# Memory's mean squares taken once, during the first projections, and kept; memory's tiles split over both output units

## The chip, the cores and the metric

The kernel runs on one core of one Trainium2 chip. The time is the device time of one launch in microseconds (us), the median over several runs. Engines are named as the profile names them: PE is TensorE's matmul queue, PEld its weight loads, DVE VectorE, ACT ScalarE, POOL GpSimd, SP the engine that issues the DMAs.

## What is computed

Two layers of an encoder on 512 tokens of width 1024. Each has a token mixer (differential attention in layer 0, dilated attention in layer 1), a cross attention into 256 memory tokens, and a squared-ReLU MLP. Every sub-layer is normalised before and after:

```python
def rms_norm(x, g):
    xf = x.astype(jnp.float32)
    y = xf * lax.rsqrt(jnp.mean(xf * xf, axis=-1, keepdims=True) + NORM_EPS)
    return (y * g.astype(jnp.float32)).astype(x.dtype)

def memory_cross_attention(h, mem, mem_g, wq, wkv, wo):
    ...
    mn = rms_norm(mem, mem_g)
    q = (h @ wq).reshape(B, S, H, Dh)
    kv = (mn @ wkv).reshape(B, M, 2, H, Dh)
    ...

for i in range(DEPTH):
    h = rms_norm(x, mix_pre_g[i])
    ...                                   # mix = the layer's token mixer
    x = x + rms_norm(mix, mix_post_g[i])
    h = rms_norm(x, xa_pre_g[i])
    x = x + rms_norm(memory_cross_attention(h, mem, mem_g[i], xa_wq[i], xa_wkv[i], xa_wo[i]), xa_post_g[i])
    h = rms_norm(x, ffn_pre_g[i])
    x = x + rms_norm(squared_relu_mlp(h, w_up[i], w_down[i]), ffn_post_g[i])
```

`mem` is the same in both layers; only its gain `mem_g[i]` and the weights `xa_wkv[i]` differ. So the mean square of each memory token is the same number in both layers.

## The kernel before, in words

Activations lie with features on the 128 partitions: eight tiles of 128 features, by 512 tokens (256 for memory). Every product of a weight is made in three matmuls of split operands (high part by high part, and the two cross terms), so each weight and each activation is split: ACT rounds it into a high part (a *head*: `heads_of`, L608, for weights), and DVE subtracts that from the original for the low part (a *rest*: `rests_of`, L1021).

Work on weights is cut into *units* of 512 output columns. A unit has four *pairs* (0 to 3); a pair is two feature tiles of the weight, 512 KB, loaded by one DMA of SP into one of four slots of `raw`. For one pair PE runs 2 x 4 x 3 = 24 matmuls of 128x512 (12 in the two first units on memory, which have two banks of 128 tokens). Before a pair PE waits for its rest. A unit leaves four PSUM banks, which ACT or DVE evacuates while PE is at the next unit (units alternate between banks 0 to 3 and 4 to 7).

The units in order: `qkv0` (6 units, the *projections* of layer 0, numbered 0 to 5 here), then differential attention, `o0` (2 units, the first and the second *output unit*), `kv0` (4 units on memory: two make values, two keys), `xq0`, cross attention, `xo0`, the MLP, and then layer 1 the same with its own projections (`qkv1a`, `qkv1b`), `o1`, `kv1`, and so on.

There is no scheduler: each engine's program is written out by hand, one after the other, and runs strictly in that order; engines meet only at semaphores. In ACT's and DVE's `unit` the order is: the heads (or rests) of pairs 2 and 3 of this unit, each followed by a call `between(0)`, `between(1)`; then pair 0 of the next unit; then the banks 0 to 3 of this unit, with pair 1 of the next unit put in after bank 1 (`second=2`), and `between(2)` and `between(3)` after banks 1 and 3. What is put in a `between` so stands in front of all later heads of that engine.

Memory's normalisation before the change, in each layer:

- SP waits until the attention has used its values (`att.weighed`), then loads `mem_sb` (L405, 1 MB), then the weights of the second output unit.
- ACT, in the first output unit between the heads of pairs 2 and 3 (`mem_squares(0)`), waits for memory and squares its eight tiles (L901). POOL adds them up into one tile (L460, 7 additions).
- PE, in the first output unit before pair 3, sums that tile over the partitions with a matmul against ones (`statistic`, L1656); ACT makes `rstd` of it (`root`, Ln and Exp, L651 and L654) after bank 1.
- In the second output unit, DVE forms each memory tile times gain times `rstd` in `stage` (two slots, `mem_tile`, L1090), ACT takes its head `mem_hi` (L659), DVE its rest `mem_lo` (L1076): tiles 0 to 2 after pair 2's rest, 3 and 4 after pair 3's, 5 and 6 after bank 1, the last after bank 3.
- The `kv` units multiply these tiles. In `kv`, before pair 2, PE also forms the statistic of the mixer's output, from `sq` tiles that ACT squares out of the banks and POOL adds up.

`mem_sb`, `mem_hi`, `mem_lo` and `mem_sq` lie in a region that the attention of either layer also uses.

## Time and profile before

| | |
|---|---|
| median of 3 runs | 1956.73 us (1955.13 to 1957.24) |
| the profiled execution's own time | 1953.03 us |
| its span, first to last instruction | 1951.2 us |
| PE busy | 1891.0 us, 97% |
| PEld busy | 1570.2 us, 80% |
| DVE busy | 1008.1 us, 52% |
| ACT busy | 727.7 us, 37% |
| POOL busy | 226.3 us, 12% |
| mean granted TensorE clock | 0.992 |
| the chain that ended last, by engine | PE 84%, DVE 8%, ACT 5%, issue 2%, POOL 1%, DMA 1% |
| DMA share of 16 engines | 27.1% |

A busy share is time in which the engine had an instruction in work, over the span. The chain is followed back from the last instruction, each step to what released it. PE's instructions overlap: a matmul of 128x512 is shown as some 390 ns, while the next one starts 227 ns later, so start times say more than durations.

### The profile page before, as it was taken

To read this page: it belongs to the slowest core of one execution; us is meant where nothing else is said; L and a number is where in the kernel's file an instruction comes from. 1 tells how busy PE (TensorE), PEld (TensorE's weight loads), DVE (VectorE), ACT (ScalarE), POOL (GpSimd) and SP (SyncE) were. 2 spreads that over 40 slices of the span, in tenths; PEclk is the share of its full clock that TensorE was granted. 3 is DMA by queue.
4 is the path that set the end of the run, shared out by engine and by line. 5 is a ranking of instruction groups with operands and counts; after the bars stand their busy time and mean duration, and the time that the engine had idled before them with its cause. 6 is when DMAs were issued, how large, how long until landed. Compare 5 with 4: busy or idle time off the path is not lost.

```text
span 1951.2 us, 25744 instructions
## 1 busy us (share of the span) xinstructions
PE 1891.0 (97%) x9874; PEld 1570.2 (80%) x9874; DVE 1008.1 (52%) x1465; ACT 727.7 (37%) x1284; POOL 226.3 (12%) x214
## 2 busy tenths in 40 slices
PE   8999999999999999999999999999899999999997
PEld 6785577889888888887888788887788898888887
DVE  5967946544644243567642366433474364333444
ACT  5126855434423142442123411234453353232232
POOL 0420021000430000103310033200300000000001
PEclk9999999999999999999999999999999999999999
DMA  4230024403232222322332123311351123232321
GB/s 160 87 107 1 1 96 139 144 12 98 67 119 89 93 86 92 114 65 76 97 111 62 34 86 97 119 33 52 101 184 54 59 72 108 87 97 86 104 80 64
DMA packets 86753, 167.46 MB, mean 86 GB/s; under 512 B 5633, under 2 KB 7809, under 8 KB 86401
## 3 DMA queue, kind: packets, MB, share of 16 engines
q1 hardware_dynamic: 86656, 166.15, 27.1%
q8 instruction: 64, 1.05, 0.2%
q14 instruction: 33, 0.26, 0.0%
HBM read 164.03 MB, written 2.10 MB: 85 GB/s over the span
## 4 chain that ended last, share of the span: by engine, by line
PE 84%; DVE 8%; ACT 5%; issue 2%; POOL 1%; DMA 1%; SPq 0%; ACTq 0%; POOLq 0%; DVEq 0%
PE ps L1597 68%; PE ps L1630 5%; DVE w_lo L1021 2%; DVE half L1068 1%; PE ps L1724 1%; PE ps L1899 1%; PE ps L1656 1%; PE ps L1768 1%; DVE small L1286 1%; PE ps L1891 1%; PE ps L1762 1%; ACT w_hi L608 1%; PE ps L1844 1%; POOL mem_sq L460 1%; PE ps L1838 1%
## 5 line engine op out<-in xcount | busy, mean ns | idle before, releaser
L1021 DVE TENSOR_TENSOR w_lo<-raw,w_hi 128x1024 fp32r<-128x1024 f32 x304 | 389.8, 1307 | 296.7 <-ACT w_hi L608 295.1
L1597 PE MATMUL ps<-act_hi,w_lo 128*128 128x512 f32 x1244 | 490.3, 394 | 5.4 <-DVE w_lo L1021 4.0
L608 ACT ACTIVATE w_hi<-raw 128x1024 fp32r<-128x1024 f32 x304 | 313.6, 1055 | 479.4 <-PE ps L1597 472.3
L1597 PE MATMUL ps<-act_lo,w_hi 128*128 128x512 f32 x1248 | 485.8, 390 | 0.0
L1597 PE MATMUL ps<-act_hi,w_hi 128*128 128x512 f32 x1244 | 484.7, 390 | 0.0
L1597 PEld LDWEIGHTS ps<-act_hi,w_lo 128*128 128x128 f32 x1244 | 233.9, 188 | 57.7 <-DVE w_lo L1021 5.9
L1597 PEld LDWEIGHTS ps<-act_lo,w_hi 128*128 128x128 f32 x1248 | 234.7, 188 | 50.1 <-issue 1.9
L1597 PEld LDWEIGHTS ps<-act_hi,w_hi 128*128 128x128 f32 x1244 | 233.9, 188 | 49.0
L1597 PE MATMUL ps<-ff_hi,w_lo 128*128 128x512 f32 x448 | 176.5, 394 | 0.0
L1597 PE MATMUL ps<-ff_lo,w_hi 128*128 128x512 f32 x448 | 176.5, 394 | 0.0
L1597 PE MATMUL ps<-ff_hi,w_hi 128*128 128x512 f32 x448 | 176.5, 394 | 0.0
L460 POOL TENSOR_TENSOR sq<-sq 128x512 f32<-128x512 f32 x26 | 41.5, 1595 | 902.8 <-ACT sq L993 564.0
L1490 DVE SCALAR_TENSOR_TENSOR half<-ps,rstd 128x512 f32<-128x512 f32 x64 | 43.6, 686 | 144.9 <-PE ps L1597 132.5
L1511 DVE TENSOR_TENSOR y_sb<-ps,y_sb 128x512 f32<-128x512 f32 x56 | 37.3, 687 | 146.6 <-PE ps L1597 146.6
L967 ACT ACTIVATE stage<-half 128x512 f32<-128x512 f32 x64 | 40.3, 630 | 193.0 <-DVE half L1490 192.9
L1068 DVE TENSOR_TENSOR half<-ps,sin_sb 64x512 f32<-64x512 f32 (+1 forms) x160 | 110.1, 688 | 2.2
L1597 PE MATMUL ps<-w_hi,act_lo 128*128 128x512 f32 x256 | 102.8, 402 | 0.0
L1597 PE MATMUL ps<-w_lo,act_hi 128*128 128x512 f32 x256 | 102.1, 399 | 0.0
L1597 PE MATMUL ps<-w_hi,act_hi 128*128 128x512 f32 x256 | 101.8, 397 | 0.0
L1597 PEld LDWEIGHTS ps<-ff_lo,w_hi 128*128 128x128 f32 x448 | 83.8, 187 | 20.8
L1597 PEld LDWEIGHTS ps<-ff_hi,w_hi 128*128 128x128 f32 x448 | 83.8, 187 | 20.8
L1597 PEld LDWEIGHTS ps<-ff_hi,w_lo 128*128 128x128 f32 x448 | 83.8, 187 | 20.6
(202 smaller groups left out, 2775.9 us busy)
## 6 DMA issues: line engine op xcount, KB each, us to landing
raw<-in_db_w_qkv SPq DMA_DIRECT2D x72, 512.0 KB, 4.0
raw<-in_w_up SPq DMA_DIRECT2D x64, 512.0 KB, 3.7
raw<-in_w_down SPq DMA_DIRECT2D x64, 512.0 KB, 3.9
raw<-in_xa_wkv SPq DMA_DIRECT2D x32, 512.0 KB, 3.9
raw<-in_da_w_qkv SPq DMA_DIRECT2D x24, 512.0 KB, 3.8
raw<-in_xa_wq SPq DMA_DIRECT2D x16, 512.0 KB, 4.4
raw<-in_xa_wo SPq DMA_DIRECT2D x16, 512.0 KB, 3.9
raw<-in_da_w_o SPq DMA_DIRECT2D x8, 512.0 KB, 4.4
```

The costliest lines, as they stand in the source:

```text
L460: nc.gpsimd.tensor_tensor(squares[:, 0, :], squares[:, 0, :], squares[:, k, :], ALU.add).then_inc(sq_summed, 1)
L608: nc.scalar.activation(w_hi[:, g % 4], raw[:, g % 4], ACT.Copy).then_inc(w_hi_ready, 1)
L967: nc.scalar.activation(stage[:, n % 2, :], half[:, n % 2, :], ACT.Square).then_inc(staged, 1)
L1021: nc.vector.tensor_tensor(w_lo[:, g % 4], raw[:, g % 4], w_hi[:, g % 4].bitcast(f32), ALU.subtract).then_inc(w_lo_ready, 1)
L1068: last = nc.vector.tensor_tensor(pieces(half[to:to + swap, m % 2:m % 2 + 1, :]), src[at:at + swap], pieces(sin_sb[at:at + swap]), ALU.mult)
L1286: nc.vector.tensor_reduce(small[:, t % 2, 2:2 + count], scores, AX.X, ALU.max, negate=True).then_inc(a.taken, 1)
L1490: nc.vector.scalar_tensor_tensor(hidden, source, 0.0, scale, ALU.max, ALU.mult).then_inc(bank_out[(u + up) % 2], 1)
L1511: nc.vector.tensor_tensor(tile, ps[:, 4 * (v % 2) + m, :], tile, ALU.add).then_inc(bank_out[v % 2], 1)
L1597: last = nc.tensor.matmul(ps[:, s + m, 0:width], left, right, start=(k == 0 and n == 0 and not early), stop=(k == KT - 1 and n == 2))
L1630: last = nc.tensor.matmul(half_bank(u, m, n), left, right, start=(k == 0 and i == 0 and m % 2 == 0), stop=(k == KT - 1 and i == 2), skip_g ...
L1656: last = nc.tensor.matmul(ps[:, stat_bank(name), 0:width], ones[:, :], squares[:, k, :], start=(k == order[0]), stop=(k == order[-1]))
L1724: last = nc.tensor.transpose(a.turn_banks(n, b), a.e[:, n % (a.lag + 1), b * P:(b + 1) * P], ident[:, :])
```

## The change

The mean squares are taken once. SP loads memory behind the weights of projection unit 3. ACT squares it behind projection unit 2's heads; POOL adds up behind its sixteen rotary sums of layer 0; PE forms the statistic before pair 2 of projection unit 5; and ACT makes `rstd_mem`, a tensor of its own that nothing overwrites, before the head of pair 0 of the first output unit. In layer 1 nothing of this is done again, but memory itself is loaded again, at the same place as before, since the region was used in between. `mem_sb` changes places with `mem_hi` and `mem_lo` in the region, so that the attention of layer 0 leaves it alone.

The splitting of memory's tiles moves forward: tiles 0 to 3 into the first output unit, behind the head and rest of pair 3 (`first_mem_heads`, `first_mem_rests`), 4 and 5 behind pair 2's and 6 and 7 behind pair 3's of the second. DVE, not ACT, now waits for memory in layer 1.

```diff
@@ SP
             for n in range(1, 6):
                 load_unit(n, w, 0, n)
+                if n == 3:
+                    sp.dma_start(mem_sb[:, :, :], mem).then_inc(mem_loaded, 16)
...
-                sp.wait_ge(att.weighed, att.n)
-                sp.dma_start(mem_sb[:, :, :], mem).then_inc(mem_loaded, 16)
+                if layer == 1:
+                    sp.wait_ge(att.weighed, att.n)
+                    sp.dma_start(mem_sb[:, :, :], mem).then_inc(mem_loaded, 16)
@@ POOL
-                for k in range(KT):
-                    square_sum(f"mem{layer}", k, mem_sq)
+                if layer == 0:
+                    for k in range(KT):
+                        square_sum("mem0", k, mem_sq)
@@ ACT
             for n in range(1, 4):
                 unit(u + n)
+                if n == 2:
+                    act.wait_ge(mem_loaded, 16)
+                    for k in range(KT):
+                        nc.scalar.activation(mem_sq[:, k, :], mem_sb[:, k, :], ACT.Square).then_inc(sq_ready, 1)
             copy_columns(u + 4, 1)
+            def memory_root(j):
+                if j == 1:
+                    root("mem0", rstd_mem)
...
-                def mem_squares(j):
-                    if j == 0:
-                        act.wait_ge(mem_loaded, 16 * (layer + 1))
-                        for k in range(KT):
-                            nc.scalar.activation(mem_sq[:, k, :], mem_sb[:, k, :], ACT.Square).then_inc(sq_ready, 1)
-                    if j == 2:
-                        root(f"mem{layer}", MEM)
+                def first_mem_heads(j):
+                    if j == 1:
+                        for k in range(4):
+                            staged_head(f"mem{layer}", k, mem_hi, MEM)
 
                 def mem_heads(j):
-                    for k in (2 * j, 2 * j + 1):
-                        staged_head(f"mem{layer}", k, mem_hi, MEM)
+                    if j < 2:
+                        for k in (4 + 2 * j, 5 + 2 * j):
+                            staged_head(f"mem{layer}", k, mem_hi, MEM)
@@ DVE
+                def first_mem_rests(j):
+                    if j == 1:
+                        dve.wait_ge(rstd_ready, STATS["mem0"] + 1)
+                        dve.wait_ge(mem_loaded, 16 * (layer + 1))
+                        for i in range(4):
+                            mem_tile(layer, i)
+
                 def mem_rests(j):
-                    if j == 0:
-                        dve.wait_ge(rstd_ready, STATS[f"mem{layer}"] + 1)
-                        mem_tile(layer, 0)
-                    for i in (2 * j + 1, 2 * j + 2):
-                        mem_tile(layer, i)
+                    if j < 2:
+                        for i in (4 + 2 * j, 5 + 2 * j):
+                            mem_tile(layer, i)
+                    if j == 1:
+                        mem_tile(layer, KT)
@@ PE
             def diff_starts():
+                pe.wait_ge(ln_done, STATS["mem0"] + 1)
...
-            unit(u + 5, act_hi, act_lo, SPLITS["pre0"], tokens=natural, before_pair={3: diff_starts})
+            unit(u + 5, act_hi, act_lo, SPLITS["pre0"], tokens=natural,
+                 before_pair={2: lambda: statistic("mem0", squares=mem_sq), 3: diff_starts})
...
                 unit(o, act_hi, act_lo, split,
-                     before_pair={1: mixer_ends, 3: lambda: statistic(f"mem{layer}", squares=mem_sq)})
-                unit(o + 1, act_hi, act_lo, split, last_bank=sums_read(f"mem{layer}"))
+                     before_pair={1: mixer_ends})
+                unit(o + 1, act_hi, act_lo, split)
```

How the instructions stand on an engine before and after. First ACT in the projections of layer 0, before (`w_hi` is a head, `v` an evacuated bank of values, `e_sb` the first exponentials of the attention):

```order
L861 ACTIVATE lam_w<-lam_w 128x2
L608 ACTIVATE w_hi<-raw 128x1024 x12
L728 ACTIVATE rstd_cols<-ps 128x8
L608 ACTIVATE w_hi<-raw 128x1024 x3
L643 ACTIVATE v<-ps,rstd_cols 128x512 x2
L608 ACTIVATE w_hi<-raw 128x1024
L643 ACTIVATE v<-ps,rstd_cols 128x512 x2
L608 ACTIVATE w_hi<-raw 128x1024 x3
L782 ACTIVATE e_sb,small<-ps,small 128x512 x2
```

The same stretch of ACT now:

```order
L865 ACTIVATE lam_w<-lam_w 128x2
L613 ACTIVATE w_hi<-raw 128x1024 x8
L871 ACTIVATE mem_sq<-mem_sb 128x256 x8
L613 ACTIVATE w_hi<-raw 128x1024 x4
L732 ACTIVATE rstd_cols<-ps 128x8
L613 ACTIVATE w_hi<-raw 128x1024 x3
L648 ACTIVATE v<-ps,rstd_cols 128x512 x2
L613 ACTIVATE w_hi<-raw 128x1024
L648 ACTIVATE v<-ps,rstd_cols 128x512 x2
L613 ACTIVATE w_hi<-raw 128x1024 x2
L656 ACTIVATE rstd_mem<-ps,eps 128x256
L659 ACTIVATE rstd_mem<-rstd_mem 128x256
```

The squares stand in front of the last four heads of projection units 3 and 4, and the root stands in front of the head of the first output unit's pair 0.

DVE from the first output unit's pair 2 to the `kv` units, before, in layer 0 (layer 1 reads the same; `w_lo` is a weight's rest, the first five are the pairs 2 and 3 of the first and 0 to 2 of the second output unit):

```order
L1021 TENSOR_TENSOR w_lo<-raw,w_hi 128x1024 x5
L1090 SCALAR_TENSOR_TENSOR stage<-mem_sb,gain,rstd 128x256 x2
L1076 TENSOR_TENSOR mem_lo<-stage,mem_hi 128x256
L1090 SCALAR_TENSOR_TENSOR stage<-mem_sb,gain,rstd 128x256
L1076 TENSOR_TENSOR mem_lo<-stage,mem_hi 128x256
L1021 TENSOR_TENSOR w_lo<-raw,w_hi 128x1024
L1090 SCALAR_TENSOR_TENSOR stage<-mem_sb,gain,rstd 128x256
L1076 TENSOR_TENSOR mem_lo<-stage,mem_hi 128x256
L1090 SCALAR_TENSOR_TENSOR stage<-mem_sb,gain,rstd 128x256
L1076 TENSOR_TENSOR mem_lo<-stage,mem_hi 128x256
L1021 TENSOR_TENSOR w_lo<-raw,w_hi 128x1024
L1090 SCALAR_TENSOR_TENSOR stage<-mem_sb,gain,rstd 128x256
```

DVE now, from the second output unit's pair 0 on (the first four tiles and three rests stand before this piece, behind the first two `w_lo`):

```order
L1032 TENSOR_TENSOR w_lo<-raw,w_hi 128x1024 x3
L1101 SCALAR_TENSOR_TENSOR stage<-mem_sb,gain,rstd_mem 128x256
L1087 TENSOR_TENSOR mem_lo<-stage,mem_hi 128x256
L1101 SCALAR_TENSOR_TENSOR stage<-mem_sb,gain,rstd_mem 128x256
L1087 TENSOR_TENSOR mem_lo<-stage,mem_hi 128x256
L1032 TENSOR_TENSOR w_lo<-raw,w_hi 128x1024
L1101 SCALAR_TENSOR_TENSOR stage<-mem_sb,gain,rstd_mem 128x256
L1087 TENSOR_TENSOR mem_lo<-stage,mem_hi 128x256
L1101 SCALAR_TENSOR_TENSOR stage<-mem_sb,gain,rstd_mem 128x256
L1087 TENSOR_TENSOR mem_lo<-stage,mem_hi 128x256 x2
L1032 TENSOR_TENSOR w_lo<-raw,w_hi 128x1024 x5
```

Before, memory's work stood on both sides of the rest of `kv`'s pair 1 (the last `w_lo` of the piece before is `kv`'s pair 0; pair 1's follows three instructions behind the end of the piece); now all of it stands in front of the five rests of `kv`'s pairs 0 to 3 and of the next unit's pair 0.

ACT in the first output unit, before:

```order
L608 ACTIVATE w_hi<-raw 128x1024
L901 ACTIVATE mem_sq<-mem_sb 128x256 x8
L608 ACTIVATE w_hi<-raw 128x1024 x2
L642 ACTIVATE sq<-ps 128x512
L643 ACTIVATE y_sb<-ps 128x512
L642 ACTIVATE sq<-ps 128x512
L643 ACTIVATE y_sb<-ps 128x512
L651 ACTIVATE rstd<-ps,eps 128x256
```

And now:

```order
L613 ACTIVATE w_hi<-raw 128x1024 x2
L663 ACTIVATE mem_hi<-stage 128x256 x4
L613 ACTIVATE w_hi<-raw 128x1024
L647 ACTIVATE sq<-ps 128x512
L648 ACTIVATE y_sb<-ps 128x512
L647 ACTIVATE sq<-ps 128x512
L648 ACTIVATE y_sb<-ps 128x512
L613 ACTIVATE w_hi<-raw 128x1024
```

Squares and root are gone from here; four heads of memory stand in front of the head of the second output unit's pair 0.

## Rows read from the trace of the kernel before

**Rows 1.** Waits of the whole run: who waited for whom, us total, times, longest.

```profile
PE ps L1597 <- DVE w_lo L1021: 9.1, 10, 2.1
```

**Rows 2.** Timeline of PE, layer 0, first output unit: start, us, instruction [idle before].

```profile
274.53 0.39 PE L1597 MATMUL ps<-act_lo,w_hi 128*128 128x512 f32 x1
274.76 0.39 PE L1597 MATMUL ps<-act_hi,w_hi 128*128 128x512 f32 x1
276.85 0.67 PE L1656 MATMUL ps<-mem_sq,ones 128*128 128x256 f32 x2 [1.70 <-POOL mem_sq L460]
...
277.59 0.40 PE L1597 MATMUL ps<-act_lo,w_hi 128*128 128x512 f32 x1
```

**Rows 3.** Timeline of PE, layer 1, the same place.

```profile
1367.95 0.39 PE L1597 MATMUL ps<-act_hi,w_hi 128*128 128x512 f32 x1
1371.55 0.67 PE L1656 MATMUL ps<-mem_sq,ones 128*128 128x256 f32 x2 [3.21 <-POOL mem_sq L460]
...
1372.29 0.40 PE L1597 MATMUL ps<-act_lo,w_hi 128*128 128x512 f32 x1
```

**Rows 4.** Timeline of POOL, layer 0, first output unit.

```profile
268.68 8.02 POOL L460 TENSOR_TENSOR mem_sq<-mem_sq 128x256 f32<-128x256 f32 x7 [143.88 <-ACT mem_sq L901]
```

**Rows 5.** Timeline of ACT, layer 1, first output unit.

```profile
1363.00 2.57 ACT L901 ACTIVATE mem_sq<-mem_sb 128x256 f32<-128x256 f32 x8 [3.59 <-DMA mem_sb<-in_mem]
```

**Rows 6.** Instructions on `mem_sb`: duration ns min/median/max, first and last start.

```profile
L1090 DVE SCALAR_TENSOR_TENSOR stage<-mem_sb,gain,rstd x16: 471/482/1504, 289.7 to 1404.2; 128x256 f32<-128x256 f32 x16
...
DMA to landing us min/median/max: 4.9/5.2/5.5
```

**Rows 7.** Timeline of PE, layer 0, `kv` pairs 0 to 2.

```profile
307.13 0.39 PE L1597 MATMUL ps<-w_hi,mem_hi 128*128 128x512 f32 x1
309.65 0.50 PE L1597 MATMUL ps<-w_hi,mem_lo 128*128 128x512 f32 x1 [2.13 <-DVE w_lo L1021]
309.99 0.40 PE L1597 MATMUL ps<-w_lo,mem_hi 128*128 128x512 f32 x1
...
314.07 0.39 PE L1597 MATMUL ps<-w_lo,mem_hi 128*128 128x512 f32 x1
```

**Rows 8.** Timeline of ACT, same stretch.

```profile
304.70 0.74 ACT L659 ACTIVATE mem_hi<-stage 128x256 fp32r<-128x256 f32 x2
305.31 1.08 ACT L608 ACTIVATE w_hi<-raw 128x1024 fp32r<-128x1024 f32 x1
```

**Rows 9.** Timeline of DVE, same stretch.

```profile
305.24 1.23 DVE L1076 TENSOR_TENSOR mem_lo<-stage,mem_hi 128x256 fp32r<-128x256 f32 x1 [8.57 <-ACT mem_hi L659]
...
307.31 2.29 DVE L1021 TENSOR_TENSOR w_lo<-raw,w_hi 128x1024 fp32r<-128x1024 f32 x1
```

**Rows 10.** Timeline of POOL, same stretch.

```profile
303.45 2.74 POOL L460 TENSOR_TENSOR sq<-sq 128x512 f32<-128x512 f32 x2 [14.76 <-ACT sq L642]
306.96 3.79 POOL L460 TENSOR_TENSOR sq<-sq 128x512 f32<-128x512 f32 x2 [0.77 <-ACT sq L642]
```

**Rows 11.** Timeline of PE, layer 1, `kv` pair 1.

```profile
1401.83 0.39 PE L1597 MATMUL ps<-w_hi,mem_hi 128*128 128x512 f32 x1
...
1407.87 0.39 PE L1597 MATMUL ps<-w_hi,mem_hi 128*128 128x512 f32 x1
```

**Rows 12.** Stretches: us, busy (x) of PE, PEld, DVE, ACT, POOL, granted clock, DMA share, GB/s.

```profile
1404.40:1407.80 3.40, 3.40 (x8) 2.72 (x9) 2.73 (x4) 2.07 (x3) 1.02 (x1) 0.50 0.49 159
309.70:313.10 3.40, 3.40 (x14) 2.50 (x14) 2.73 (x4) 2.04 (x3) 1.04 (x1) 1.00 0.47 154
```

**Rows 13.** Timeline of SP, projections, first load of unit 4.

```profile
79.93 0.37 SPq L382 DMA_DIRECT2D raw<-in_da_w_qkv  x1
```

**Rows 14.** Timeline of DVE, projections, rest of unit 3's pair 2.

```profile
94.70 1.23 DVE L1021 TENSOR_TENSOR w_lo<-raw,w_hi 128x1024 fp32r<-128x1024 f32 x1
```

**Rows 15.** Timeline of POOL, projections, last rotary sum.

```profile
122.47 2.33 POOL L532 TENSOR_TENSOR k<-k,half 128x512 f32<-128x512 f32 x1 [2.46 <-DVE half L1068]
```

**Rows 16.** Timeline of PE, first scores of the attention.

```profile
150.47 1.99 PE L1762 MATMUL ps<-k,q 64*128 64x512 f32 x8
```

More of the change, by code:

```diff
@@ L200, in build @@
         eps = sb("eps", [P, 1])
+        rstd_mem = sb("rstd_mem", [P, MEM])
         rstd_cols = sb("rstd_cols", [P, 2 * DIL])
@@ L645, in copies, with root @@
                 unit(u, bank, nb=nb, between=between, second=second, first_steps=first_steps)
-            def root(name, width=S):
-                n = STATS[name]
+            def root(name, dst=rstd):
+                n, width = STATS[name], dst.shape[-1]
                 act.wait_ge(stat_done, n + 1)
-                nc.scalar.activation(rstd[:, 0:width], ps[:, stat_bank(name), 0:width], ACT.Ln,
+                nc.scalar.activation(dst[:, :], ps[:, stat_bank(name), 0:width], ACT.Ln,
                                      bias=eps[:, 0:1], scale=1.0 / D).then_inc(ln_done, 1)
                 act.wait_ge(ln_done, n + 1)
-                nc.scalar.activation(rstd[:, 0:width], rstd[:, 0:width], ACT.Exp,
-                                     scale=-0.5).then_inc(rstd_ready, 1)
+                nc.scalar.activation(dst[:, :], dst[:, :], ACT.Exp, scale=-0.5).then_inc(rstd_ready, 1)
             def staged_head(name, k, dst, width=S):
@@ L863, in _ @@
                 unit(u + n)
+                if n == 2:
+                    act.wait_ge(mem_loaded, 16)
+                    for k in range(KT):
+                        nc.scalar.activation(mem_sq[:, k, :], mem_sb[:, k, :], ACT.Square).then_inc(sq_ready, 1)
             copy_columns(u + 4, 1)
+            def memory_root(j):
+                if j == 1:
+                    root("mem0", rstd_mem)
             for n in range(2):
                 copies(u + 4 + n, lambda m, n=n: v0[:, m, n * NB:(n + 1) * NB],
-                       scale=lambda m: rstd_cols[:, m:m + 1], first_steps=(att_d, exp_diff, 2) if n == 1 else None)
+                       scale=lambda m: rstd_cols[:, m:m + 1], first_steps=(att_d, exp_diff, 2) if n == 1 else None,
+                       between=memory_root if n == 1 else None)
             attention(att_d, exp_diff, 2, (2, diff_out), (5, diff_root), (7, diff_head))
@@ L1422, in _ @@
                 u = UNITS[f"o{layer}"]
-                def mem_rests(j):
-                    if j == 0:
-                        dve.wait_ge(rstd_ready, STATS[f"mem{layer}"] + 1)
-                        mem_tile(layer, 0)
-                    for i in (2 * j + 1, 2 * j + 2):
-                        mem_tile(layer, i)
-                unit(u)
+                def first_mem_rests(j):
[4 more added lines that the diff above has]
+                            mem_tile(layer, i)
+                def mem_rests(j):
+                    if j < 2:
[3 more added lines that the diff above has]
+                        mem_tile(layer, KT)
+                unit(u, between=first_mem_rests)
                 unit(u + 1, between=mem_rests)
```

12 lines of the change are left out of this document (6 added, 6 removed).

## The prediction

> **What bounds the kernel now.** I read the page first: PE is in work 97% of the span, and 84% of the chain that ended last is PE's, most of it L1597, the matmuls on weights. So only what PE does, or waits for, counts, and I looked for PE's idle time around the instructions that move. The list of waits says that the matmuls on weights wait ten times for a rest, 9.1 us in all, 2.1 at the longest [rows 1]. The timeline of PE puts the costly places on the map. In the first output unit PE stops in front of memory's statistic for POOL's sum: 1.70 us in layer 0, 3.21 in layer 1 [rows 2, 3]. In `kv` it stops 2.13 us in front of pair 1 for the rest of that pair [rows 7], and in layer 1 the same wait is followed by a stretch at half clock, 0.50, which is 1.2 GHz, while in layer 0 the clock stayed at 1.00, 2.4 GHz [rows 12]. In the steady state a matmul starts every 0.227 us (274.53 to 274.76, 0.23 as rounded) [rows 2].
>
> **Term 1, layer 0, first output unit.** Without statistic, the first matmul of pair 3 would start at 274.99 and the second at 275.21. The second starts at 277.59 [rows 2]. Both the wait and the statistic leave this place: 2.38 us. What is late next is the rest of pair 3. Its head stood behind the 2.57 us of squares (the same eight in layer 1) [rows 5]; it now stands where the squares stood, before POOL began at 268.68 [rows 4], so head (1.1, rows 8) and rest (1.2, rows 14) are done by 271, four us ahead of PE.
>
> **Term 2, layer 1, same place.** The second matmul would start at 1367.95 + 2 x 0.227 = 1368.40 and starts at 1372.29 [rows 3]: 3.89 us, the statistic with it, which in layer 1 isn't done again. The new wait here is DVE's for memory. Memory has landed at 1363.00, when ACT stopped waiting for it [rows 5]. Behind that wait DVE has four products and three rests of tiles: 4 x 0.48 [rows 6] and 3 x at most 1.23 (what such a rest took beside a busy POOL [rows 9]; POOL is idle here), 5.6 us, until 1368.6. Then come the head (1.1) and the rest (1.2) of the second output unit's pair 0, ready at 1370.9 at the latest. PE starts pair 3 at 1368.2 and, after 24 x 0.227 = 5.45 us, wants that rest at 1373.6: 2.7 us of cover at least, and some 4 if the rests of tiles take as long as the products. In layer 0 nothing is waited for and the cover is larger. I price this at nothing; if memory landed more than 4 us later, each us more would be PE's.
>
> **Term 3, the statistic in the projections.** It is a matmul PE has to do somewhere: from its start at 276.85 to the second matmul behind it at 277.59 are 0.74 us, where plain matmuls take 0.23, so 0.51 [rows 2], paid before pair 2 of unit 5. Bounds: 0.23, one more start, and 1.4, what the mixer's statistic of 512 columns cost in `kv` (314.07 - 309.99 - 12 x 0.227 [rows 7]). I take 0.51, the same matmul. Does it wait? PE does pair 2 of unit 5 directly in front of the first scores, at 150.47 [rows 16], so it reaches the statistic at 150.47 - 5.45 = 145.0. SP issues memory just ahead of the load that went out at 79.93 [rows 13]; with 5.5 us at most to landing [rows 6] it is there by 85.5, squared by 88.1. POOL's last rotary sum ends at 124.80 [rows 15], and seven additions took 8.02 us [rows 4]: 132.8, 12 us ahead of PE. ACT then makes the root at 145.6 to 146.6, within pair 2's 5.45 us, so the scores don't wait for it. Behind the root stands one head, for a pair PE wants a hundred us later, and its rest gets done before DVE has the first scores to reduce. The squares hold up ACT's head of unit 3's pair 2 to about 89.2; its rest is DVE's at 94.70 [rows 14], so 5.5 us of cover. The 1 MB also delays the next weights by some 3 us in a queue whose heads come 10 us after the issue. Cost: 0.5 us, nothing else.
>
> **Term 4, `kv` in layer 0.** ACT's head of pair 1 starts at 305.31 because two heads of memory stand in front, from 304.70 [rows 8]; DVE's rest starts only at 307.31, behind three operations on memory of which the first took 1.23 us, and itself takes 2.29 instead of 1.23 [rows 9, 14]. POOL is adding squares meanwhile, from 303.45 to 306.19 and again from 306.96 [rows 10]. With memory gone, the head starts at 304.70, ends at 305.75, and the rest can begin at 305.85. If it is held up until POOL's addition ends at 306.19 and then runs its 1.23, it is ready at 307.4, and PE wants it at 307.36. The second matmul of pair 1 would start at 307.13 + 2 x 0.227 = 307.58 and starts at 309.99 [rows 7]: 2.4 us. Pair 2 has a little more: of the 1.4 us that the mixer's statistic cost there, at most 1.0 is its own (twice the columns of memory's, at 0.51), so some 0.5 is a wait for pair 2's rest, whose head stood behind memory's last tile. Of the 2.9 I take off 0.3 for what the two rests are still late: 2.6 us. Bounds: 0.7 (rival A) and 2.9.
>
> **Contention, told apart.** Rows 9 and 10 show a DVE operation with two inputs in SBUF lengthened while POOL adds. The Trainium skill, "SBUF — State Buffer", section "Who interferes with whom", says that such an operation and a GpSimd one that reads SBUF exclude each other for a whole instruction, the later one blocking. By that rule the rest begins when the addition in work ends, as I have it; had POOL's third addition got in first, it would be rival A.
>
> **Term 5, `kv` in layer 1.** The wait is the same 2.13; then the half clock. From 1401.83, the ninth matmul of pair 1 would start 9 x 0.227 later, at 1403.88; it starts at 1407.87 [rows 11]: 3.99 us, of which 2.4 is the wait with its restart and 1.6 the clock. I count both, less 0.3: 3.7. That the low stretch goes with the wait is a choice: it begins as PE resumes.
>
> **The sum.** 2.38 + 3.89 - 0.51 + 2.6 + 3.7 = 12.1 us. Everything behind shifts as a whole: the loads follow the rests by semaphore, and the list of waits has PE wait for no load. The profiled execution took 1953.03 us (span 1951.2, 1.8 around it), so it would take 1940.9. It lies 3.7 under the median of 1956.73; I carry the difference along: 1956.7 - 12.1 = 1944.6 us.
>
> **Rivals.**
> A. `kv` keeps its wait. POOL's third addition gets ahead of the rest of pair 1 (squares are now ready earlier, too). The rest then begins at about 306.3 + 1.6 = 307.9 and is ready at 309.1: 0.7 us won per layer, and the half clock stays. Terms 1 to 3 make 5.8, so 5.8 + 1.4 = 7.2: 1949.5. For it: the 2.29 us of rows 9, and another arrival of squares. Against it: the third square can't be ready before 306.2, when DVE already stands in line.
> B. The clock falls elsewhere. The same 2.13 us wait was followed by 0.50 in one layer and by 1.00 in the other [rows 12], so what PE did just before doesn't fix it. If the stretch in layer 1 stays, 1946.2; with one or two new ones at 1.6 each, up to 1949.4. The other way, if runs nearer the median had more of them behind waits that go, up to three: 1940. The Trainium skill, "TensorE: Matmul & The Clock Gate", section "What's actually happening", has the clock judged by recent activity in a free-running window, so that the place of a fall differs between runs; by it the 1.6 is not firm: 1946.2 without it.
> C. The wait comes back in the second output unit. Memory lands late in layer 1, DVE and ACT both stand behind it, and the rest of pair 0 is late. It takes 4 + 8 us of delay to bring the change within 0.2% of before, 1952.8 to 1960.6; against it stand the landings, 4.9 to 5.5 [rows 6].
> D. Slower: ACT's wait for memory in the projections. It stands in front of the heads of units 3 and 4. From 5.5 us of delay of the landing on, PE pays each us; slower by over 0.2% needs 12.1 + 3.9 = 16 us paid, so a landing 21 us late: above 1960.6, say 1962. Only a DMA queue much fuller than the traced one could do it.
>
> **Numbers.** Forecast 0.70; A 0.12; B 0.11; C 0.05; D 0.02. A measurement of this kernel tells about 0.2%, 3.9 us, from no change. Faster by more: forecast, A and B, 0.93; same 0.05; slower 0.02. The range: 1940 (three more half-clock stretches gone) to 1951 (A with one more such stretch, 1949.5 + 1.6).
>
> **What would show it.** In the changed profile: the matmuls of pair 3 in both first output units follow pair 2's at 0.23 us; no POOL work in front of PE there; memory's statistic in unit 5 with no idle time, first scores at 151.0; PE's idle time before `kv` pair 1 under 0.5 us, and the rest of that pair starting within 1.2 us of its head's start; PE's output-to-`kv` stretch 4.5 us shorter in layer 0, 7.6 in layer 1. PE idle before the statistic in unit 5, before the second output unit's pair 0, or before unit 3's pair 2 would show it wrong.

## The result, and the profile after

The changed kernel takes 1939.74 us (median of 4 runs, 1937.45 to 1940.82) against 1956.97 us before (4 runs on the same chip, 1955.13 to 1957.24): the ratio is 0.9912, with a 95% interval of 0.9895 to 0.9930 (13.7 to 20.5 us). The forecast was 1944.6 us in a range of 1940 to 1951: faster, as said, but 17.2 us are won where 12.1 were forecast, and the time lies 0.3 us under the range. The list of terms held; what was too small is the price of TensorE's clock behind the waits that went. The win in medians is itself uncertain by a us or so: over the 31 executions of before on one chip that the first experiments brought, 13 took 1952.3 to 1955.3 us and 18 took 1956.3 to 1958.7, so the median of a few falls in one group or the other (12 of them had 1956.90, the other 19 had 1955.20).

The profiled execution after took 1937.45 us. From its profile, first the span, the busy times and the chain:

```profile
span 1935.7 us, 25717 instructions
PE 1885.3 (97%) x9872; PEld 1567.4 (81%) x9872; DVE 1003.7 (52%) x1465; ACT 724.9 (37%) x1274; POOL 218.0 (11%) x207
PE 86%; DVE 7%; ACT 4%; issue 2%; DMA 0%; SPq 0%; ACTq 0%; DVEq 0%
```

The waits of the whole run, for the row of [rows 1]:

```profile
PE ps L1615 <- DVE w_lo L1032: 5.1, 9, 1.6
```

9.1 us have become 5.1, and the two waits of 2.1 us are gone. PE's timeline (start, us, instruction, [idle before]), first where memory's statistic stood in the first output unit of layer 0 [rows 2], then the statistic at its new place in projection unit 5, then `kv` of layer 0 [rows 7]: the last matmul of pair 0, the first two of pair 1, and the second of pair 2:

```profile
275.13 0.39 PE L1615 MATMUL ps<-act_hi,w_hi 128*128 128x512 f32 x1
275.36 0.39 PE L1615 MATMUL ps<-act_hi,w_lo 128*128 128x512 f32 x1
275.58 0.39 PE L1615 MATMUL ps<-act_lo,w_hi 128*128 128x512 f32 x1
...
145.24 0.60 PE L1674 MATMUL ps<-mem_sq,ones 128*128 128x256 f32 x2
145.49 0.58 PE L1615 MATMUL ps<-w_hi,act_lo 128*128 128x512 f32 x1
...
305.07 0.39 PE L1615 MATMUL ps<-w_hi,mem_hi 128*128 128x512 f32 x1
305.30 0.47 PE L1615 MATMUL ps<-w_hi,mem_lo 128*128 128x512 f32 x1
305.61 0.40 PE L1615 MATMUL ps<-w_lo,mem_hi 128*128 128x512 f32 x1
...
309.28 0.40 PE L1615 MATMUL ps<-w_lo,mem_hi 128*128 128x512 f32 x1
```

No bracket stands behind any of them: PE waits at none of these places. ACT, DVE and POOL around `kv` pair 1 of layer 0 [rows 8 to 10]:

```profile
302.64 1.09 ACT L613 ACTIVATE w_hi<-raw 128x1024 fp32r<-128x1024 f32 x1
...
303.76 1.45 DVE L1032 TENSOR_TENSOR w_lo<-raw,w_hi 128x1024 fp32r<-128x1024 f32 x1 [8.90 <-ACT w_hi L613]
...
301.39 2.74 POOL L464 TENSOR_TENSOR sq<-sq 128x512 f32<-128x512 f32 x2 [15.58 <-ACT sq L647]
304.29 3.51 POOL L464 TENSOR_TENSOR sq<-sq 128x512 f32<-128x512 f32 x2 [0.16 <-ACT sq L647]
```

The rest starts 1.12 us after its head and is ready at 305.21 (303.76 + 1.45), just as PE comes to it. The stretches where the two `kv` waits and, in the middle row, PE's wait for POOL in layer 1 had been, for [rows 12] (us, busy (x) of PE, PEld, DVE, ACT, POOL, granted clock, DMA share, GB/s):

```profile
305.30:308.60 3.30, 3.30 (x15) 2.52 (x14) 1.95 (x1) 2.27 (x3) 2.36 (x2) 1.00 0.47 159
1364.00:1367.40 3.40, 3.40 (x16) 2.82 (x15) 0.15 (x1) 3.19 (x6) 1.30 (x1) 1.00 0.05 19
1390.60:1394.00 3.40, 3.40 (x15) 2.47 (x14) 2.10 (x1) 2.21 (x3) 2.33 (x2) 1.00 0.46 154
```

All are at 2.4 GHz. I set the starts of the same matmuls in the two first profiled executions side by side. The table has what PE is ahead by at a point, and what the step before it brought. In `kv` of layer 0, for example, PE is 307.13 - 305.07 = 2.06 us ahead at the last matmul of pair 0 and 314.07 - 309.28 = 4.79 at the second of pair 2, a step of 2.7:

| place | ahead | step | forecast |
|---|---|---|---|
| behind the statistic in projection unit 5 | -0.8 (-0.4 from 166 us on) | -0.46 | -0.51 |
| layer 0, behind the first output unit's pair 2 | 2.0 | 2.4 | 2.38 |
| layer 0, behind `kv` pair 2 | 4.8 | 2.7 | 2.6 |
| a half-clock stretch near 848 half as long, one at 1346 gone | 7.6 | 2.8 | - |
| layer 1, behind the first output unit's pair 2 | 11.5 | 3.9 | 3.89 |
| layer 1, behind `kv` pair 2 | 15.3 | 3.8 | 3.7 |
| end of the span | 15.5 | | |

The five terms make 12.4 us here, 12.1 forecast. (The expectations below say 12.7, and 3.0 for term 4; by the starts of the same matmuls they are 12.4 and 2.7.) These two executions differ by 15.6 us; the medians differ by 17.2.

### The profile page after: what moved, and what is told of

The parts are those of the page before. It is cut to its first block, busy times and chain, and to the rows that moved or that the text cites. A ratio compares the mean times of both kernels' runs of the same rounds, so it can differ in the third digit from the quotient of the medians.

```text
span 1935.7 us, 25717 instructions
## 1 busy us (share of the span) xinstructions
PE 1885.3 (97%) x9872; PEld 1567.4 (81%) x9872; DVE 1003.7 (52%) x1465; ACT 724.9 (37%) x1274; POOL 218.0 (11%) x207
## 4 chain that ended last, share of the span: by engine, by line
PE 86%; DVE 7%; ACT 4%; issue 2%; DMA 0%; SPq 0%; ACTq 0%; DVEq 0%
PE ps L1615 70%; PE ps L1648 6%; DVE w_lo L1032 2%; DVE half L1079 1%; PE ps L1742 1%; PE ps L1919 1%; PE ps L1674 1%; PE ps L1780 1%; PE ps L1786 1%; PE ps L1911 1%; DVE small L1297 1%; ACT w_hi L613 1%; PE ps L1864 1%; PE ps L1858 1%; PE ps L1849 1%
```

## The experiments

Ratios are against the kernel before, run on the same chip; an interval is of 95%. The last four experiments ran on another chip, where before had a median of 1953.47 us (7 runs) and the changed kernel wasn't run: there the times can't be set beside the changed kernel's 1939.23 to a us, and ratios and traces say more. "PE is ahead" or "behind" is read from the starts of the same matmuls.

**The two kernels again.** No edit; both were run again, each with a further profile.

> The kernel before, unchanged, for more executions and a second trace. Theory 1 (the 4.5 us by which the change won more than the 12.7 of its terms are half-clock stretches of TensorE that come and go from run to run, and the kernel before has more of them): the profiled execution of before was a lucky one; the times here lie at 1955 to 1957.5, their recorded mean clock falls with the time, about 0.001 for each 1.9 us (0.990 where the time is 1957, 0.992 where it is 1953), and a trace of a slower execution has one to three half-clock stretches of 3.4 us more than the six inside the first trace, most of them where PE resumes after a wait. Theory 2 (the difference is in work or waits that the trace shows at full clock): the clock does not go with the time, and a second trace shows the same stretches with longer waits.

> The changed kernel, unchanged, for more executions and a second trace. Theory 1: 1937 to 1941, clock 0.994 to 0.995, again falling with the time; four to five half-clock stretches before the last 20 us, at the same kinds of places (columns in the projections, start of the attention, the MLP's end, columns in layer 1). Theory 2: the same times with no relation to the clock.

Before: 1956.90 us (12 runs, 1953.22 to 1958.73), ratio 1.0006 [0.9997, 1.0014]. Changed: 1939.23 us (5 runs, 1937.29 to 1940.75), ratio 0.9917 [0.9903, 0.9931]. In the 12 executions of before the mean clock goes with the time, as the first theory said: 0.990 or 0.991 in the nine that took 1956.3 us and more, 0.992 or 0.993 in the three under 1955.4. The second profile of before is longer than the first by 4.4 us (span 1955.6), and this is where. PE at the three places (the waits, then the stretches behind them):

```profile
309.80 0.50 PE L1597 MATMUL ps<-w_hi,mem_lo 128*128 128x512 f32 x1 [2.13 <-DVE w_lo L1021]
1373.11 1.19 PE L1656 MATMUL ps<-mem_sq,ones 128*128 128x256 f32 x2 [3.08 <-POOL mem_sq L460]
1408.76 0.50 PE L1597 MATMUL ps<-w_hi,mem_lo 128*128 128x512 f32 x1 [2.13 <-DVE w_lo L1021]
```

```profile
310.90:314.20 3.30, 3.30 (x9) 2.54 (x8) 2.63 (x5) 2.31 (x3) 0.00 (x0) 0.50 0.45 152
1372.50:1379.00 6.50, 5.89 (x14) 4.67 (x15) 0.00 (x0) 0.00 (x0) 0.46 (x1) 0.50 0.32 105
1409.90:1413.30 3.40, 3.40 (x10) 2.63 (x9) 2.73 (x5) 2.31 (x3) 0.00 (x0) 0.50 0.47 151
```

The waits are as long as in the first profile, but here all three are followed by 1.2 GHz; there one was [rows 12]. Against the first profile PE loses 1.1 us at the first and 2.7 us at the second, 3.8 of the 4.4 us that its last matmuls are apart. The rest nearly cancels: 0.9 us in the first 20 us and 0.4 near 850, less 0.7 near 162, where the first profile has a half-clock stretch and the second has none. The 3.8 us are as large as the 3.7 between the first profile's time and the median, which the prediction had carried along.

**The kernel before three times more, the changed one once more**, a single execution each.

> The kernel before, unchanged, once more with a profile. Theory: its executions differ by how many of the three long waits that the change removes in kv (both layers) and in layer 1's first output unit (2.13, 3.1 and 2.13 us) are followed by a stretch of PE at a granted clock of 0.50, each costing 1.6 us; one had one such stretch and a span of 1951.2, the other had three and 1955.6. A span near 1951 should then show one or none behind these waits, one near 1955.5 two or three; the other low stretches (near 111, 848, 991, 1346 and at the end) should be the same in either. Rival: the number behind these waits is one or two throughout, and the spans differ by stretches elsewhere.

> As the run before this one: theory, the span follows the number of half-clock stretches behind the three removed waits, 1.6 us each, from about 1949.6 for none to 1955 for three; rival, it follows stretches elsewhere.

> A further execution of the kernel before, for the count: over the profiled executions with these three waits I expect a low stretch behind more than half of the waits of 2 us and above, and behind none of the 1.70 us ones.

> The changed kernel, unchanged, once more with a profile. Theory: no low stretch between 270 and 335 us and none between 1355 and 1415 us, where no wait over 0.3 us is left; its span, 1935.7 and 1938.9 so far, varies by the stretches at 111, 844, 985, 1342 and the end alone. Rival: low stretches come where they like, and one stands in these parts too.

All five executions of before that were profiled, in order of time, and the three of the changed kernel; the columns say whether 1.2 GHz followed the wait:

| execution | own time | span | `kv`, layer 0 (2.13 us) | PE for POOL, layer 1 (3.1 to 3.2) | `kv`, layer 1 (2.13) |
|---|---|---|---|---|---|
| before, first | 1953.03 | 1951.2 | no | no | yes |
| before, third | 1953.24 | 1951.4 | no | no | yes |
| before, fifth | 1955.10 | 1953.3 | no | yes | yes |
| before, fourth | 1956.39 | 1954.6 | yes | yes | yes |
| before, second | 1957.41 | 1955.6 | yes | yes | yes |
| changed, three | 1937.45, 1940.75, 1940.80 | 1935.7, 1938.9, 1939.1 | no wait, 1.00 | no wait, 1.00 | no wait, 1.00 |

The stretches of the fourth behind the first two waits, both low:

```profile
309.50:312.80 3.30, 3.30 (x9) 2.52 (x9) 2.63 (x4) 2.10 (x3) 0.89 (x1) 0.50 0.50 159
1371.50:1377.50 6.00, 5.24 (x12) 4.13 (x13) 0.00 (x0) 0.00 (x0) 0.61 (x1) 0.50 0.35 125
```

The time goes up with the count, as the theory said; the rival's "one or two throughout" is refuted. The low clock followed 10 of these 15 waits, more than half, as expected, and none of the five of 1.70 us in layer 0's first output unit. The price was not the expected 1.6 each: beside the executions without it, it was 1.1 us in `kv` of layer 0 and 2.6 to 2.7 behind the wait for POOL. The low stretches elsewhere are not the same in all five either, so this part of my expectation fell: the second, fourth and fifth have none near 162 (0.7 us), the fifth none near 111 (1.6 us), and the first 20 us differ by up to 1.4 us. In the changed kernel none stands between 270 and 335 or 1355 and 1415 us, in any of three.

**Only the kept statistic**, tiles split at their old places.

```diff
-                def first_mem_rests(j):
-                    if j == 1:
+                def mem_rests(j):
+                    if j == 0:
                         dve.wait_ge(rstd_ready, STATS["mem0"] + 1)
                         dve.wait_ge(mem_loaded, 16 * (layer + 1))
-                        for i in range(4):
-                            mem_tile(layer, i)
+                        mem_tile(layer, 0)
+                    for i in (2 * j + 1, 2 * j + 2):
+                        mem_tile(layer, i)
```

> The statistic kept as in the change, but memory's tiles split where they were before. By the prediction's terms 1 to 3: 5.9 us below before in work and waits (2.39 + 3.86 - 0.35), kv keeps its waits of 2.1 us in front of pair 1 in both layers: 3.0 and 2.4 us above the change in these. Theory 1: beyond that, clock stretches behind the two kept waits in some runs, so 1946 to 1951 in time, mean clock 0.992 to 0.994. Rival (the early splitting gives nothing by itself, and kv's wait is a matter of POOL's additions): within 1 us of the change, 1939 to 1941.

1946.79 us (5 runs), ratio 0.9959 [0.9946, 0.9972]. The time lies in the range of the first theory. PE's waits for POOL are gone, both waits in `kv` are there, and the last again with a granted clock of 0.50 behind it. PE, then DVE and POOL in front of the first, then the stretch behind the last:

```profile
307.34 0.50 PE L1603 MATMUL ps<-w_hi,mem_lo 128*128 128x512 f32 x1 [2.13 <-DVE w_lo L1026]
1398.11 0.50 PE L1603 MATMUL ps<-w_hi,mem_lo 128*128 128x512 f32 x1 [2.13 <-DVE w_lo L1026]
...
305.00 2.29 DVE L1026 TENSOR_TENSOR w_lo<-raw,w_hi 128x1024 fp32r<-128x1024 f32 x1
...
304.64 3.78 POOL L464 TENSOR_TENSOR sq<-sq 128x512 f32<-128x512 f32 x2 [0.77 <-ACT sq L647]
```

```profile
1398.70:1402.00 3.30, 3.30 (x9) 2.62 (x8) 2.63 (x4) 2.31 (x3) 0.49 (x1) 0.50 0.53 159
```

So terms 1 and 2 belong to the statistic alone, terms 4 and 5 to the place of the tiles.

**Only the tiles' place.** The kernel before, its statistic formed in each layer as before, with all eight tiles split behind pairs 2 and 3 of the second output unit (four each).

```diff
-                    for k in (2 * j, 2 * j + 1):
-                        staged_head(f"mem{layer}", k, mem_hi, MEM)
+                    if j < 2:
+                        for k in range(4 * j, 4 * j + 4):
+                            staged_head(f"mem{layer}", k, mem_hi, MEM)
```

> The other part alone: both layers take their statistic as before, but tiles 0 to 3 are split behind pair 2 and tiles 4 to 7 behind pair 3 of the second output unit. By terms 4 and 5: kv's wait goes in both layers, 3.0 + 2.4 us, the waits of 1.7 and 3.2 us for POOL in the first output unit stay. Theory 1: 5.4 us below before plus a share of the clock's, so 1948 to 1952. Rival: the four tiles in front of pair 3's rest and the next pairs delay the second output unit, and PE waits there instead: not below 1955.

1948.13 us (8 runs), ratio 0.9970 [0.9959, 0.9980], as the first theory had it. PE keeps its waits for POOL and loses those in `kv`; a new one, which was not expected, stands before the mixer's statistic of layer 1:

```profile
275.83 0.67 PE L1659 MATMUL ps<-mem_sq,ones 128*128 128x256 f32 x2 [1.70 <-POOL mem_sq L460]
1367.79 0.67 PE L1659 MATMUL ps<-mem_sq,ones 128*128 128x256 f32 x2 [3.32 <-POOL mem_sq L460]
1402.12 1.10 PE L1659 MATMUL ps<-sq,ones 128*128 128x512 f32 x2 [0.86 <-POOL sq L460]
```

Each part alone wins 0.41% and 0.30%; both together 0.83% on this chip. The sum, 0.71%, agrees with 0.83% within the intervals, so these runs show no interaction of the two parts. They don't exclude one either: this kernel has the tiles at other places than the change, and the new wait is not in the change.

**The statistic of layer 1 done again** in the changed kernel, its result unused.

```diff
+                    if j == 0 and layer == 1:
+                        act.wait_ge(mem_loaded, 32)
+                        for k in range(KT):
+                            nc.scalar.activation(mem_sq[:, k, :], mem_sb[:, k, :], ACT.Square).then_inc(sq_ready, 1)
+                    if j == 2 and layer == 1:
+                        root("mem1", rstd[:, 0:MEM])
@@ PE
-                     before_pair={1: mixer_ends})
+                     before_pair={1: mixer_ends, **({3: lambda: statistic("mem1", squares=mem_sq)} if layer else {})})
```

> The change, but layer 1 takes its statistic again where it did before (squares, POOL's additions, PE's statistic before pair 3, the root), though its result is not used: tiles still take the kept root and are still split early. Theory 1: PE waits 3.2 us for POOL again in layer 1's first output unit, 3.9 us in all with the statistic (term 2), kv stays without a wait in both layers, and in some executions a half-clock stretch of 1.6 us follows that wait: 1943 to 1945 against the changed kernel's 1939.2. Rival: the squares in front of pair 3's head delay the early tiles too, and the second output unit's pair 0 comes late as well: 1945 or more.

1944.16 us (4 runs), ratio 0.9948 [0.9931, 0.9965], in the range of the first theory, but the wait is 2.46 us and not 3.2. In the profile PE falls behind the changed kernel by 4.8 us at this place, of which 1.6 are the clock. The two waits, POOL's last addition in front of the second, and the stretch behind the first:

```profile
1363.35 1.16 PE L1681 MATMUL ps<-mem_sq,ones 128*128 128x256 f32 x2 [2.46 <-POOL mem_sq L466]
1399.29 1.10 PE L1681 MATMUL ps<-sq,ones 128*128 128x512 f32 x2 [0.85 <-POOL sq L466]
...
1396.95 2.19 POOL L466 TENSOR_TENSOR sq<-sq 128x512 f32<-128x512 f32 x1 [0.44 <-POOL sq L466]
```

```profile
1363.40:1366.80 3.40, 3.40 (x8) 2.72 (x9) 2.10 (x6) 1.78 (x3) 0.00 (x0) 0.50 0.16 60
```

The second wait was not expected. It is the one of the kernel with only the tiles moved: both have memory's statistic in layer 1 and the tiles early. The trace shows how POOL comes to be late. Its last addition begins 0.44 us behind the one before, where the changed kernel has 0.14. DVE's rest of pair 2 has by then been in work for 0.16 us, and the addition takes 2.19 us; in the changed kernel it begins 0.13 us ahead of that rest and takes 1.30. The gap of 0.44 stands at this place in all seven profiled executions with memory's statistic in layer 1, those of before too, and in none of the seven without; why POOL has it then is open.

**Memory's load of layer 1 put behind the second output unit's weights.**

```diff
+                load_unit(u + 1, w, 0, 1)
                 if layer == 1:
                     sp.wait_ge(att.weighed, att.n)
                     sp.dma_start(mem_sb[:, :, :], mem).then_inc(mem_loaded, 16)
-                load_unit(u + 1, w, 0, 1)
```

> The change, but layer 1's memory is loaded behind the weights of the second output unit, not in front, so it lands some 5 us later. Its first tile product now starts at 1355.6 and would start at 1361; the rest of the second output unit's pair 0 was ready at 1361.2 with PE wanting it at 1365.8, 4.6 us of cover. Theory (cover as the prediction's term 2 has it): PE waits about 0.5 to 1 us there in layer 1, nothing elsewhere, 1939 to 1941. Rival: ACT's evacuation of the banks and kv's rests are pushed too, the wait in kv returns and the loss is 2 us or more.

1944.28 us (4 runs), ratio 0.9953 [0.9936, 0.9970]: I had expected 1939 to 1941, and missed. The rival's loss of 2 us or more is there, but not by its way: no wait in `kv` returned. SP's issue, DVE's first tile, DVE's rest of the second output unit's pair 0, and PE, in layer 1; first the changed kernel, then this one:

```profile
1349.90 0.34 SPq L409 DMA_DIRECT2D mem_sb<-in_mem  x1
...
1355.59 0.89 DVE L1101 SCALAR_TENSOR_TENSOR stage<-mem_sb,gain,rstd_mem 128x256 f32<-128x256 f32 x2 [1.21 <-issue]
...
1360.00 1.23 DVE L1032 TENSOR_TENSOR w_lo<-raw,w_hi 128x1024 fp32r<-128x1024 f32 x1 [1.09 <-ACT w_hi L613]
```

```profile
1354.29 1.20 SPq L410 DMA_DIRECT2D mem_sb<-in_mem  x1
...
1362.44 0.88 DVE L1101 SCALAR_TENSOR_TENSOR stage<-mem_sb,gain,rstd_mem 128x256 f32<-128x256 f32 x2 [8.59 <-issue]
...
1366.85 1.23 DVE L1032 TENSOR_TENSOR w_lo<-raw,w_hi 128x1024 fp32r<-128x1024 f32 x1 [1.09 <-ACT w_hi L613]
...
1368.17 0.47 PE L1615 MATMUL ps<-act_hi,w_lo 128*128 128x512 f32 x1 [2.50 <-issue]
```

The load is issued 4.4 us later and takes 8.15 instead of 5.7 us until DVE has its first tile, behind two loads of weights issued just ahead (at 1352.7 and 1353.9). That makes the rest of pair 0 6.85 us late. In the changed kernel it is ready at 1361.2 and PE wants it at 1365.8, 4.6 us of cover. PE is 0.5 us earlier in this execution, so 6.85 + 0.5 - 4.6 = 2.8 us should be lost, and PE lost 2.8 by its starts (2.50 in the bracket). The prediction's cover ("2.7 at least, some 4") holds as a lower bound; my expectation had the delay at 5 us and left out the clock. Behind this wait, too, a granted clock of 0.50 followed, from 1369.6 on, and cost 1.6 us.

**Tiles 6, 7 and the last rest put back behind bank 1** of the second output unit, in both layers.

```diff
-                    if j < 2:
-                        for i in (4 + 2 * j, 5 + 2 * j):
+                    if j in (0, 2):
+                        for i in (4 + j, 5 + j):
                             mem_tile(layer, i)
-                    if j == 1:
+                    if j == 2:
                         mem_tile(layer, KT)
```

> The change, but memory's last two tiles (6 and 7, and the last rest) stand behind bank 1 of the second output unit, in front of the rest of kv's pair 1, in both layers. Theory (order: what is put in front of that head and rest is what made PE wait, with POOL's additions lengthening it): PE waits 1.5 to 2.5 us in front of kv's pair 1 in both layers, and pair 2 less than before: 1943 to 1945, with a half-clock stretch behind one of the waits in some executions. Rival (the wait came from the tile behind bank 3 and from the split of tile 4 in a blocked DVE alone): under 0.5 us, 1939 to 1940.

1942.29 us (4 runs), ratio 0.9934 [0.9918, 0.9951]. PE's waits in `kv` come back with 0.47 us, not with 1.5 to 2.5; the rival had the size of the wait. The time lies between the two forecasts, and its ratio can't be told from the changed kernel's 0.9917 [0.9903, 0.9931]; the reading rests on the trace. PE, DVE and POOL in layer 0:

```profile
306.33 0.50 PE L1615 MATMUL ps<-w_hi,mem_lo 128*128 128x512 f32 x1 [0.47 <-DVE w_lo L1032]
...
305.07 1.21 DVE L1032 TENSOR_TENSOR w_lo<-raw,w_hi 128x1024 fp32r<-128x1024 f32 x1
...
305.30 3.58 POOL L464 TENSOR_TENSOR sq<-sq 128x512 f32<-128x512 f32 x2 [0.77 <-ACT sq L647]
```

Set beside the kernel with only the statistic kept, this takes the wait of 2.13 us apart. There the rest starts 2.00 us after its head (303.00 to 305.00), here 1.41 (303.66 to 305.07), since in front of it stand the rests of two tiles, and not two rests and the product of a further tile: 0.59. There POOL's addition had begun 0.36 us ahead of the rest, which took 2.29; here the rest was 0.23 ahead of POOL, and took 1.21: 1.08. Together 1.67, and the waits differ by 1.66. The last 0.47 come with the heads and rests of two tiles in front. No low clock follows the waits of 0.47.

**A step on.** Apart from the wait at the start of the program, the changed kernel's longest waits for a rest are one of 1.63 us in the MLP (at 884) and two in the projections of layer 0, where DVE has the rest behind two rotary banks of five operations each, 7.0 us. DVE, then PE, in the changed kernel:

```profile
64.48 2.79 DVE L1079 TENSOR_TENSOR half<-ps,sin_sb 32x512 f32<-32x512 f32 x4
67.30 1.23 DVE L1032 TENSOR_TENSOR w_lo<-raw,w_hi 128x1024 fp32r<-128x1024 f32 x1
...
68.58 0.50 PE L1615 MATMUL ps<-act_hi,w_lo 128*128 128x512 f32 x1 [1.25 <-DVE w_lo L1032]
91.62 0.50 PE L1615 MATMUL ps<-act_hi,w_lo 128*128 128x512 f32 x1 [0.96 <-DVE w_lo L1032]
```

One rest was put before each rotary bank there:

```diff
-                           4 * n, DA_DQ // 2, scaling=scalings_at.get(n), done=(2, 4, 3, 3)[n], ahead=3 if n else 4,
-                           second=2 if n else 0, between=angles_between(0) if n == 0 else None)
-            unit(u + 4, done=3)
+                           4 * n, DA_DQ // 2, scaling=scalings_at.get(n), done=4 if n else 2, ahead=4,
+                           second=1 if n else 0, between=angles_between(0) if n == 0 else None)
+            unit(u + 4, done=4)
```

> The change, and in the projections of layer 0 DVE's four rests of the next unit stand one before each rotary bank, instead of one before bank 0, one after bank 1 and one after bank 2 with the last in the next unit. In the changed kernel PE waits 1.25 us for the rest of unit 2's pair 1 and 0.96 us for that of unit 3's. Theory (order again): both waits go with their restarts, 2.4 us, none comes back, and with them any half-clock stretch they cause: 1936.5 to 1937.5. Rival (DVE has too much to do there: four banks of 3.5 us and four rests of 1.25 against 21.8 us of PE; the waits only move to pair 2 or to the banks): 1938.5 to 1939.5.

1935.91 us (4 runs, 1934.64 to 1936.88), ratio 0.9905 [0.9888, 0.9921], the lowest time of all, and 0.6 us under the range of the theory. Both waits are gone, and PE's waits for a rest make 2.6 us in the list of waits, where the changed kernel has 5.1. From 66 to 95 us PE wins 2.8 us on the changed kernel; 1.7 us of its lead are lost further on, 1.3 of them in the two later units on memory of each layer, where matmuls of 256 columns start 0.117 us apart and in the changed kernel 0.113; the reason is open. So "none comes back" holds for the waits, not for the time. As a ratio to before it can't be told from the changed kernel, since the intervals overlap.

## Why the prediction was too small

**Terms 1 and 2** (2.38 and 3.89) were measured at 2.4 and 3.9. The second matmul of pair 3 stands where the steady 0.227 us puts it (275.13 + 2 x 0.227 = 275.58). The new wait, DVE's for memory in layer 1, cost nothing; its cover was 4.6 us.

**Term 3** (-0.51) was -0.46. ACT waited for memory and POOL ended far ahead of PE:

```profile
84.56 2.57 ACT L871 ACTIVATE mem_sq<-mem_sb 128x256 f32<-128x256 f32 x8 [9.06 <-DMA mem_sb<-in_mem]
...
125.19 6.99 POOL L464 TENSOR_TENSOR mem_sq<-mem_sq 128x256 f32<-128x256 f32 x7
...
145.88 0.47 ACT L656 ACTIVATE rstd_mem<-ps,eps 128x256 f32<-128x256 f32 x1 [8.00 <-PE ps L1674]
```

POOL ended at 132.2 (forecast 132.8), 13 us before the statistic; the squares ended at 87.1 (88.1). The first scores came at 151.2 (151.0). Rival D, whose mark was a late landing here, is out: memory came at 84.6.

**Term 4** (2.6) was 2.7: of the 0.3 us that I took off for rests still late, 0.2 were there. 2.3 us came at pair 1 and 0.4 at pair 2. The mark "4.5 us shorter in layer 0" did not follow from the sum, where terms 1 and 4 make 5.0; it was 5.1. The mechanism was as told: the head ran straight behind the banks, at 302.64. The rest started 0.37 us before POOL's first two additions ended at 304.13 and was 0.22 us slower for it (1.45 for 1.23). The prediction had **contention told apart** with the rule of the Trainium skill, "SBUF — State Buffer", section "Who interferes with whom". By that rule, the trace agrees: the rest that started 0.23 us ahead of POOL took 1.21, the one 0.36 behind it 2.29. Rival A, POOL getting ahead and the wait staying, did not come: in the changed kernel the rest started 0.53 us ahead of POOL's third addition (303.76 against 304.29), and even with tiles 6 and 7 in front of it 0.23 ahead.

**Term 5** (3.7, of it 1.6 for the clock) was 3.8 between the first two profiles, 2.3 for the wait and 1.5 for the clock. The choice made there, that the low stretch goes with the wait, was right: it stood behind this wait in all five executions of before and in the one with only the statistic kept, and in none of the eight where this wait is gone or at most 0.47 us.

**The step that failed is in the sum**: "It lies 3.7 under the median of 1956.73; I carry the difference along". The difference was no constant. In the two profiled executions nearest the median (1956.39 and 1957.41) two further half-clock stretches stand behind the waits in `kv` of layer 0 and in the first output unit of layer 1, at 1.1 and 2.7 us, and the change takes them away with the waits. With both the forecast would have been 12.1 + 3.8 = 15.9, and 1940.8. The terms bring 0.3 more. Some 1.0 us of the 17.2 is not assigned; it is of the size of what the choice of executions moves (the means of the 31 executions of before and the nine of the changed kernel are 16.4 us apart). That unprofiled executions of 1957 us have the same two stretches is inferred from their mean clock of 0.990, not seen.

Rival B had this as its other way, "if runs nearer the median had more of them behind waits that go, up to three: 1940", inside a case of 0.11 which it shared with the clock falling the other way. It is what happened, with two and not three. The range had the same gap at its lower end: 1940 left room for 4.6 us (three stretches at 1.6), and 3.8 for two stretches, 0.3 from the terms and the 1.0 not assigned made 5.1.

The Trainium skill, "TensorE: Matmul & The Clock Gate", section "What's actually happening", has the clock judged in a free-running window; by it the place where the clock changes shifts between executions of one kernel. In that the trace agrees: the low clock followed the 2.13 us wait of layer 0 in 2 of 5 executions of before.

**Rival C**, the wait in the second output unit, did not come; the kernel with memory's load put back makes it, and 2.8 us of delay beyond the cover then cost 2.8, and 1.6 for the clock.

## What to carry to other kernels

- Before a profile's time is set beside a median, ask what the slower executions have more of. Where the difference is clock that falls behind waits, a change that removes the waits removes the difference as well, and it belongs to the sum, not to what is carried along. One further profile of a slower execution of before, taken ahead of the forecast, could have shown it.
- What stands in front of a late rest can cost more than its durations: one product of a memory tile less (0.48 us) took 0.6 us off by itself, and 1.1 more since the rest then got in ahead of POOL's addition.
- A value that does not depend on the layer is best formed where the engines that make it have cover. Here a statistic that cost 2.4 and 3.9 us in the output units costs some 0.5 in the projections.

## What the runs showed of the hardware

- A wait of PE of 2.1 to 3.3 us amid matmuls was followed by a granted clock of 0.50 in 13 of 20 cases over the profiled executions: 6 of 6 in `kv` of layer 1, 2 of 6 in `kv` of layer 0, 3 of 6 in the first output unit of layer 1, and both waits of 2.46 and 2.50 us in the two experiments. Beside executions or kernels without it, it cost 1.1 us in `kv` of layer 0, 1.5 in `kv` of layer 1, 1.6 in the two experiments, where it lasted 3.4 us, and 2.6 to 2.7 in the output unit of before, where it lasted 6.8 us: more than half of the wait itself.
- Length alone does not decide, nor is a wait needed. Near 111 and 991 us the clock fell to 0.50 in 10 and 13 of the 14 profiled executions, and in none of these does a wait of PE over 0.1 us stand in the 5 us ahead. A wait of 1.63 us in the MLP, near 885, was followed by it in none of the 14. Of the six waits of 1.7 us in layer 0's first output unit none was followed by it. A wait of the same length at the start of the attention, near 161, was followed by it in 6 of the 14; in the changed kernel once in three. Here are the stretches behind this wait (1.69 us in both) in its first and in its second profile:

```profile
161.90:165.20 3.30, 3.30 (x12) 1.47 (x11) 2.88 (x5) 1.94 (x5) 0.00 (x0) 0.50 0.45 159
```

```profile
163.00:166.00 3.00, 2.04 (x12) 0.93 (x11) 2.93 (x5) 1.94 (x5) 0.00 (x0) 1.00 0.61 175
```

- In layer 1 the load of memory (1 MB) took 5.7 us from its issue to the first instruction on it when it went ahead of the weights, and 8.15 when two loads of weights were issued just ahead of it.
- DVE operations and POOL additions with inputs in SBUF held each other up by order of arrival: a rest that began 0.36 us behind an addition took 2.29 us instead of 1.23, one that began 0.23 us ahead took 1.21, and an addition that began 0.16 us behind a rest took 2.19 instead of 1.30.
